# Latent attention scores as split products, with the embedded input kept in DRAM meanwhile

## The reference, cut to what matters

```python
def first_block(x, p, positions, ...):
    x = layer_norm(x, ln_emb_g, ln_emb_b)              # the "embedded input"
    z = x @ w_in[i]
    xs, gs, cq, ckv, kr, gm = jnp.split(z, IN_SPLIT_POINTS, axis=-1)
    ys = s5_branch(xs, ...) * silu(gs)
    ym = mla_branch(cq, ckv, kr, cos, sin, ...) * silu(gm)
    mix = concatenate([ys, ym]) @ w_out[i]
    u = DEEPNORM_ALPHA * x + mix                       # the embedded input again
    ple = sigmoid(u @ w_pg[i]) * (p[i] @ w_pp[i])
    return layer_norm(u + ple, ln_g[i], ln_b[i])

def mla_branch(...):                                   # 4 heads
    q = rms_norm(cq) @ w_uq                            # per head 128 plain + 64 rotary rows
    kv = rms_norm(ckv) @ w_ukv                         # per head 128 plain key rows + 128 value rows
    k_rope = rotary(kr, cos, sin)                      # 64 rows, shared by the heads
    s = einsum(q, k) * scale                           # contraction over 128 + 64 rows
    s = where(key_pos <= q_pos, s, -inf)               # causal
    return softmax(s) @ v
```

## Time and profile before

| | us |
|---|---|
| three runs | 2280.39, 2281.03, 2282.52 |
| their median | 2281.03 |
| span of the profiled execution, first to last instruction | 2278.5 |
| PE busy over the span | 2194.5 (96%) |
| DVE, ACT, POOL busy | 1154.4, 754.5, 1192.3 |

### The profile page before, as it was taken

The page is one execution under the profiler, slowest core; times in us unless marked ns, Lnnn a source line. Parts: engine busy times, 40 slices in busy tenths (PEclk is TensorE's granted clock), DMA queues, the critical chain, the costliest instruction groups (busy, mean ns, idle before and its releaser), DMA issues.

```text
span 2278.5 us, 27616 instructions
## 1 busy us (share of the span) xinstructions
PE 2194.5 (96%) x10944; PEld 1609.4 (71%) x10944; DVE 1154.4 (51%) x1473; ACT 754.5 (33%) x1161; POOL 1192.3 (52%) x809
## 2 busy tenths in 40 slices
PE   6999999999999899999999999998999999999998
PEld 2454464676886687568866788876788888888886
DVE  6950844551186611550036724775966666652434
ACT  4121042332112511650036343135555555531211
POOL 2533510204787265435656765365688888844442
PEclk8999999999999999999999999999999999999999
DMA  3336232001223422101211235233122222154111
GB/s 134 111 74 104 84 85 70 4 19 47 92 84 98 143 65 84 34 10 37 89 25 51 83 111 194 87 144 130 47 62 82 83 82 84 64 182 157 47 37 74
DMA packets 62590, 187.73 MB, mean 82 GB/s; under 512 B 14903, under 2 KB 17255, under 8 KB 62415
## 3 DMA queue, kind: packets, MB, share of 16 engines
q1 hardware_dynamic: 50688, 143.30, 19.6%
q10 hardware_dynamic: 8688, 32.26, 3.8%
q0 software_dynamic: 3088, 10.43, 2.4%
HBM read 150.15 MB, written 33.59 MB: 81 GB/s over the span
## 4 chain that ended last, share of the span: by engine, by line
PE 89%; DVE 5%; ACT 3%; issue 2%; POOL 1%; DMA 1%; ACTq 0%; DVEq 0%
PE ps L3005 21%; PE ps L2651 16%; PE ps L2616 14%; PE ps L3124 10%; PE ps L2929 4%; PE ps L3038 3%; PE ps L325 3%; PE ps L3076 2%; PE ps L493 1%; PE ps L481 1%; PE ps L348 1%; PE ps L2731 1%; PE ps L607 1%; PE ps L618 1%; PE ps L630 1%
## 5 line engine op out<-in xcount | busy, mean ns | idle before, releaser
L1390 POOL TENSOR_TENSOR w_parts<-front,sb_zero 128x1024 fp32r<-128x1024 f32 x69 | 139.0, 2014 | 300.8 <-PE ps L3124 117.7
L3124 PE MATMUL ps<-ffn_parts,w_parts 128*128 128x512 f32 x1008 | 230.3, 389 | 1.5 <-DVE front L2577 1.5
L1463 POOL TENSOR_TENSOR up_parts<-front,up_parts 128x512 fp32r<-128x512 f32 x120 | 194.5, 1629 | 69.5 <-ACT up_parts L1736 69.5
L2616 PE MATMUL ps<-front 128*128 128x512 f32 x512 | 225.5, 599 | 2.7 <-ACT front L892 2.7
L1395 POOL TENSOR_TENSOR w_parts<-front,w_parts 128x1024 fp32r<-128x1024 f32 x75 | 207.6, 2769 | 22.5 <-ACT w_parts L1891 7.5
L3124 PEld LDWEIGHTS ps<-ffn_parts,w_parts 128*128 128x128 f32 x1008 | 189.0, 188 | 41.7 <-issue 2.6
L1300 POOL TENSOR_TENSOR front<-front,sb_csilu 128x1024 f32<-128x1024 f32 x48 | 104.3, 2172 | 210.5 <-DMA front<-w_ada 210.5
L3005 PE MATMUL ps<-t_high,up_parts 128*128 128x512 f32 x640 | 204.8, 391 | 4.9 <-ACT back L1743 4.9
L2651 PE MATMUL ps<-h_high,w_parts 128*128 128x512 f32 x672 | 187.6, 394 | 0.6 <-PE ps L2929 0.6
L2616 PEld LDWEIGHTS ps<-front 128*128 128x128 f32 x512 | 96.5, 191 | 118.6 <-issue 118.1
L3005 PE MATMUL ps<-h_high,up_parts 128*128 128x512 f32 x480 | 154.5, 389 | 1.5 <-DVE back L2345 1.5
(11 more groups left out here) (399 smaller groups left out, 4510.6 us busy)
## 6 DMA issues: line engine op xcount, KB each, us to landing
front<-w_ada SPq DMA_DIRECT2D x48, 512.0 KB, 3.6
front<-w_up SPq DMA_DIRECT2D x44, 512.0 KB, 4.4
front<-w_down SPq DMA_DIRECT2D x22, 512.0 KB, 3.6
front<-w_in SPq DMA_DIRECT2D x16, 512.0 KB, 3.6
front<-w_out SPq DMA_DIRECT2D x16, 512.0 KB, 4.7
residual<-back ACTq DMA_DIRECT2D x2, 4096.0 KB, 15.6
front<-w_gates SPq DMA_DIRECT2D x16, 512.0 KB, 4.0
gates<-back SPq DMA_DIRECT2D x16, 512.0 KB, 3.2
```

The costliest lines, as they stand in the source:

```text
L1390: pool.tensor_tensor(high, raw, zero[:, 0:1].to_broadcast((P, PAGE)), ALU.add)\
L1463: pool.tensor_tensor(parts[:, BANK:], src, parts[:, 0:BANK].bitcast(F32), ALU.subtract)\
L2616: mm = pe.matmul(ps[:, bank + nt, :], ring[:, slot, at + k * step:at + k * step + P], rhs(k0 + k)[:, nt * BANK:(nt + 1) * BANK], start=sta ...
L3124: mm = pe.matmul(ps[:, 2 * m + nt, :], parts[n % 2 + w_][:, at:at + P], half_of(AR[kk % 4 + x_], nt), start=k == 0 and q == 0, stop=k == N ...
```

## The change

Scores. Each plain key and query tile now exists twice: `KNH`, `QNH` (high, copied by ACT from PSUM as `fp32r`) and `KNL`, `QNL` (low, by DVE: PSUM minus high). Each score range becomes five `fp32r` matmuls into one accumulation: QNH*KNH, QNH*KNL, QNL*KNH over 128 rows; then `QRS`*`KRH` over 128 rows, where `QRS` of a head holds the high part of its 64 rotary query rows in one half and their low part in the other, and `KRH` the high part of the rotated keys in both halves; then the high query half against `KRL`, the low part of the keys, over 64 rows. A range is at least 256 columns wide: item 0 of each head is widened from 128 to 256 columns and item 4 from 640 to 768 (the softmax still reads w columns).

Room. The low parts lie on pages 4 to 11, where `XN` is. So ACT sends `XN` to DRAM (4 MB) after the first layer norm, DVE waits for that before the first low key part, and POOL fetches it back after the last scores have been transposed (`mla_turned` 32); DVE waits for it ahead of L2219. Two pages of the later projections move (`MH[1]` from 46 to 14, `UH[2]` from 14 to 41). The zero fill of `QR` (L2172) goes.

Waits. PE reuses a bank pair in the key and query stages only when DVE's low part is made too (`k_low`, `q_low`). Several semaphores become one running count each (`ONE_COUNT`); `T(name, n)` gives the semaphore and the shifted count, and replaces `S(name), n` at each of their waits.

The diff, without the remaining lines that only put `T(...)` for `S(...)`:

```diff
@@ -55,14 +55,25 @@
 N_VEC = _at
+ONE_COUNT = {"kv_tile": ("z_tile", 16), "q_tile": ("z_tile", 28), "qr_tile": ("z_tile", 32), "glu_tile": ("z_tile", 34),
+             "pp_tile": ("z_tile", 38), "wo_tile": ("z_tile", 46), "pg_tile": ("z_tile", 54),
+             "kv_free": ("z_free", 16), "q_free": ("z_free", 28), "yg_ready": ("z_free", 32), "glu_sig": ("z_free", 36),
+             "pp_free": ("z_free", 40)}
 def program(nc, t, out):
     with ExitStack() as ctx:
         sems = {}
         def S(name):
+            name = ONE_COUNT.get(name, (name, 0))[0]
             if name not in sems:
                 sems[name] = ctx.enter_context(nc.semaphore(name))
             return sems[name]
+        def T(name, n):
+            return S(name), ONE_COUNT[name][1] + n if name in ONE_COUNT else n
...
@@ -144,9 +155,12 @@
-        QN, QR, KN = pages(28, 4), pages(32, 4), pages(36, 4)
+        QNH, QNL = rounded_pages("q_high", 28, 4), rounded_pages("q_low", 4, 4)
+        KNH, KNL = rounded_pages("k_high", 36, 4), rounded_pages("k_low", 8, 4)
+        QRS = rounded_pages("q_rot_parts", 32, 4)
+        KRH, KRL = rounded_pages("k_rot_high", 44, 1)[0], rounded_pages("k_rot_low", 46, 1)[0]
         VT = pages(40, 4).rearrange("p k (a d) -> p (k a) d", a=2)
-        KROT, CM = page(44), page(45)
+        CM = page(45)
         COS, SIN = page(48), page(49)
...
+        xn_dram = nc.dram_tensor("embedded", (P, FT, SEQ), F32, kind="Internal").ap()
...
@@ -196,9 +211,9 @@
         WR_LAST = rounded_pages("w_parts_last", 42, 2)
         WR_1 = rounded_pages("w_parts_1", 36, 4)
-        MH, ML = rounded_pages("mix_high", (15, 46, 48, 49, 42, 43, 44, 45), 8), \
+        MH, ML = rounded_pages("mix_high", (15, 14, 48, 49, 42, 43, 44, 45), 8), \
             rounded_pages("mix_low", (16, 17, 18, 19, 24, 25, 26, 27), 8)
-        UH, UL = rounded_pages("u_high", (12, 13, 14, 20, 21, 22, 23, 40), 8), \
+        UH, UL = rounded_pages("u_high", (12, 13, 41, 20, 21, 22, 23, 40), 8), \
             rounded_pages("u_low", (16, 17, 18, 19, 24, 25, 26, 27), 8)
         WR_PG = rounded_pages("w_parts_pg", (48, 49), 2)
...
@@ -436,11 +451,15 @@
                 for qb in range(8):
                     w = (qb + 1) * P
                     q = slice(qb * P, (qb + 1) * P)
-                    sc = []
-                    for c0 in range(0, w, BANK):
-                        c1 = min(w, c0 + BANK)
-                        sc.append((c0, c1, QN[:, h, q], KN[:, h, c0:c1], True, False))
-                        sc.append((c0, c1, QR[:, h, q], KROT[:, c0:c1], False, True))
+                    sc, half = [], slice(64 * (h % 2), 64 * (h % 2) + 64)
+                    wide = 256 if qb == 0 else 768 if qb == 4 else w
+                    for c0 in range(0, wide, BANK):
+                        c1 = min(wide, c0 + BANK)
+                        sc.append((c0, c1, QNH[h][:, q], KNH[h][:, c0:c1], True, False))
+                        sc.append((c0, c1, QNH[h][:, q], KNL[h][:, c0:c1], False, False))
+                        sc.append((c0, c1, QNL[h][:, q], KNH[h][:, c0:c1], False, False))
+                        sc.append((c0, c1, QRS[h][:, q], KRH[:, c0:c1], False, False))
+                        sc.append((c0, c1, QRS[h][half, q], KRL[half, c0:c1], False, True))
                     items.append((sc, CM[:, SEQ - w:SEQ], w,
                                   lambda k, h=h: VT[:, k, h * P:(h + 1) * P], P,
                                   OBUF[h % 2][:, qb, :]))
...
@@ -1354,6 +1373,8 @@
             for k in range(2):
                 pool.wait_ge(S("mla_turned"), 30 + k)
                 pool.dma_start(PT_IN[k], t["pT"][k * P:(k + 1) * P, :]).then_inc(S("p_landed"), 16)
+            pool.wait_ge(S("mla_turned"), 32)
+            pool.dma_start(XN, xn_dram).then_inc(S("xn_back"), 16)
             pool.wait_ge(S("mla_out"), 32)
             def split(b, i=0, per=0):
...
@@ -1518,6 +1539,9 @@
             norm_act(act, "ln_emb", FT, lambda k: XN[:, k, :], lambda k: XN[:, k, :],
                      lambda k: V("ln_emb_g", k), lambda k: V("ln_emb_b", k), 0, True, TEMPS_1)
+            act.wait_ge(S("norm_ready"), tiles_to("ln_emb", FT))
+            act.dma_start(xn_dram, XN).then_inc(S("xn_in_dram"), 16)
+
             def z(tile, dst, func):
                 act.wait_ge(S("z_tile"), tile + 1)
                 src = two(2 * (tile % 2))
...
@@ -1586,22 +1610,22 @@
                     latent_gain_act(act, 2)
             for m in range(4):
-                act.wait_ge(S("kv_tile"), m + 1)
-                act.activation(KN[:, m, :], two(2 * (m % 2)), ACT.Copy).then_inc(S("kv_free"), 1)
+                act.wait_ge(*T("kv_tile", m + 1))
+                act.activation(KNH[m], two(2 * (m % 2)), ACT.Copy).then_inc(S("kv_free"), 1)
             ada_read(0, 16)
             for kt in range(8):
-                act.wait_ge(S("kv_tile"), 4 + kt + 1)
+                act.wait_ge(*T("kv_tile", 4 + kt + 1))
                 act.activation(VT[:, kt, :], ps[:, kt % 4, :], ACT.Copy).then_inc(S("kv_free"), 1)
             act.wait_ge(S("y_in_dram"), 16 * STEP)
...
             for m in range(4):
-                act.wait_ge(S("q_tile"), m + 1)
-                act.activation(QN[:, m, :], two(2 * (m % 2)), ACT.Copy).then_inc(S("q_free"), 1)
+                act.wait_ge(*T("q_tile", m + 1))
+                act.activation(QNH[m], two(2 * (m % 2)), ACT.Copy).then_inc(S("q_free"), 1)
...
@@ -2169,27 +2193,37 @@
             link(dve.memset(CM, 0.0))
             dve.sem_inc(S("dve_step"), 1)
-            link(dve.memset(QR, 0.0))
+
+            dve.wait_ge(S("xn_in_dram"), 16)
+            dve.wait_ge(S("z_tile"), 16)
+            for m in range(4):
+                dve.wait_ge(*T("kv_free", m + 1))
+                dve.tensor_tensor(KNL[m], two(2 * (m % 2)), KNH[m].bitcast(F32), ALU.subtract).then_inc(S("k_low"), 1)
             dve.wait_ge(S("kr_landed"), 64)
             dve.wait_ge(S("ssm_ps"), 32)
-            tt(KROT, page(46), COS, ALU.mult)
-            tt(page(46), page(47), SIN, ALU.mult)
-            tt(KROT, KROT, page(46), ALU.add)
+            tt(page(46), page(46), COS, ALU.mult)
+            tt(page(47), page(47), SIN, ALU.mult)
+            tt(page(46), page(46), page(47), ALU.add)
+            link(dve.tensor_copy(KRH, page(46)))
+            tt(KRL, page(46), KRH.bitcast(F32), ALU.subtract)
+            for m in range(4):
+                dve.wait_ge(*T("q_free", m + 1))
+                dve.tensor_tensor(QNL[m], two(2 * (m % 2)), QNH[m].bitcast(F32), ALU.subtract).then_inc(S("q_low"), 1)
             for m in range(2):
-                dve.wait_ge(S("qr_tile"), m + 1)
+                dve.wait_ge(*T("qr_tile", m + 1))
+                tt(page(47), two(4 * m), COS, ALU.mult)
+                tt(page(22), two(4 * m + 2), SIN, ALU.mult)
+                dve.sem_inc(S("qr_free"), 1)
+                tt(page(47), page(47), page(22), ALU.add)
                 for i in range(2):
-                    h = slice(64 * i, 64 * i + 64)
-                    tt(QR[h, 2 * m + i, :], two(4 * m)[h, :], COS[h, :], ALU.mult)
-                tt(page(46), two(4 * m + 2), SIN, ALU.mult)
-                dve.sem_inc(S("qr_free"), 1)
-                for i in range(2):
-                    h = slice(64 * i, 64 * i + 64)
-                    tt(QR[h, 2 * m + i, :], QR[h, 2 * m + i, :], page(46)[h, :], ALU.add)
+                    own, other = slice(64 * i, 64 * i + 64), slice(64 - 64 * i, 128 - 64 * i)
+                    link(dve.tensor_copy(QRS[2 * m + i][own, :], page(47)[own, :]))
+                    tt(QRS[2 * m + i][other, :], page(47)[own, :], QRS[2 * m + i][own, :].bitcast(F32), ALU.subtract)
             dve.sem_inc(S("dve_step"), 1)
             def gated(m):
-                dve.wait_ge(S("glu_sig"), m + 1)
+                dve.wait_ge(*T("glu_sig", m + 1))
                 tt(page(20 + m % 2), page(20 + m % 2), YF[:, m, :], ALU.mult)
             def gated_state(m):
...
@@ -2214,8 +2248,9 @@
             for k in range(4):
                 dve.wait_ge(S("gm_high"), k + 1)
                 dve.tensor_tensor(ML[4 + k], GM[:, k, :], MH[4 + k].bitcast(F32), ALU.subtract).then_inc(S("gm_split"), 1)
+            dve.wait_ge(S("xn_back"), 16)
             for m in range(8):
-                dve.wait_ge(S("wo_tile"), m + 1)
+                dve.wait_ge(*T("wo_tile", m + 1))
                 dve.scalar_tensor_tensor(XN[:, m, :], XN[:, m, :], ALPHA, two(2 * (m % 2)),
                                          ALU.mult, ALU.add).then_inc(S("u_ready"), 1)
             for k in range(8):
...
@@ -2745,32 +2780,36 @@
             block_landed(B_UKV)
             for m in range(4):
                 if m >= 2:
-                    pe.wait_ge(S("kv_free"), m - 1)
+                    pe.wait_ge(*T("kv_free", m - 1))
+                    pe.wait_ge(S("k_low"), m - 1)
                 tile(2 * (m % 2), b % RING, lambda k: CKV, kts=1, at=m * P).then_inc(S("kv_tile"), 1)
```

(52 more changed lines are left out.)

## The result

The changed kernel takes 2284.76 us (median of 15 runs, 2282.82 to 2286.11), the kernel before on the same chip 2280.75 us (15 runs, 2278.19 to 2282.52). The ratio is 1.0018 [1.0010, 1.0026]: 4.0 us slower by the medians. By the ratio's interval that is slower by 0.1 to 0.3%. The profiled executions are 2281.2 and 2278.5 us long, 2.7 us apart. The profiled execution of the changed kernel took 2283.47 us and is one of the six shorter ones of its fifteen (2282.82 to 2284.18 us, mean granted clock 0.988 or 0.989); the other nine took 2284.54 to 2286.11 us at 0.985 or 0.986.

The account below looks back on a forecast made before the run. PE was taken to bound the kernel (89% of the chain of waits). Attention -0.9, key stage +2.3 and query stage +1.3 sum to +2.7 us: span 2281.2, plus 2.5 from span to median, 2283.7 us; range 2272 to 2294.

Parts of the forecast that it names:

- Matmul prices: Attention scores: fp32r matmuls cost 0.229 us at 512 columns, 0.175 at 384, 0.120 at 256; 17.9 us back.
- The switch: Scores' fifth matmul, 64 rows between 128: 0.39 us per range for changing row count, 48 ranges, 18.7 us.
- Attention: Scores +0.8 us in sum, less 1.7 us hidden in PE's idle time at head changes: -0.9 us.
- Item 0's rise: First score item of a head grows from 0.43 to 0.99 us, hidden in idle time at three head changes: -1.7.
- Key stage: PE waits for DVE's subtraction before reusing bank pairs; the values start at 333.1 instead of 330.8: +2.3 us.
- Query wait: After the fourth query tile PE waits for DVE's subtraction (1.22 + 0.1 us) beyond ACT's copy: +1.3 us.
- The embedded input: Transfer to DRAM until 60 us, back near 527 us, both hidden with 6 and 30 us of cover: nothing.
- DVE's longer way: DVE's rotary writes grow some 3 us a pair, ending near 380; attention needs them at 400: hidden.
- a free switch: Rival, scores: row-count changes cost nothing for fp32r, giving 18.7 us, 2265.0 us; chance 0.10.
- dear narrow matmuls: Rival, scores: fp32r matmuls under 512 columns are no cheaper than 512, 10.9 us more, 2294.6 us; chance 0.13.
- a late transfer: Rival, embedded input: late weight block near 60 us or late return adds up to 10 us; chance 0.03.
- The half price: Rival, scores: only the drain shows at a row-count change, load hidden, 9.4 us less, 2274.3 us; chance 0.12.

Follow-up runs that it names:

- the round trip alone: The kernel before with only the embedded input's way out to DRAM and back added: 2280.75 us, ratio 1.0001 to the kernel before.
- values early: The changed kernel with the first two value tiles waiting only for the third low key part, the third for the fourth: 2280.93 us.
- rotary tile early: The changed kernel with the first rotary tile waiting only for the third low query part, its second half for the fourth: 2282.30 us.
- the last experiment: The changed kernel with 128-row fifth matmul, early rotary tile, three bank pairs, and state-space output regrouped by row count: 2257.81 us, 0.9910 to the kernel before.

## Why the prediction was right

The forecast was 2283.7 us and the same within 0.2%; 2284.8 came out, and the profiled span on the forecast's 2281.2. That the span agrees to 0.1 us is luck: errors of 1.6 and 1.7 us cancelled, and two small differences outside the forecast (-0.66 ahead, +0.6 behind) did too. The 2.5 us that the forecast added to the span was the median less the span of one execution. In the runs on record each time is 2.0 to 2.2 us above its own span for the kernel before, and 2.2 to 2.3 for the changed one. Point by point:

- Matmul prices: right. 0.23 at 512 columns, 0.175 to 0.177 at 384, 0.118 at 256, as assumed from the earlier trace rows. From their first start to the transposes items 4 to 7 take 2.51, 2.51, 2.78 and 3.09 us; 2.53, 2.53, 2.80 and 3.07 follow from the forecast's prices. They agree so well because the first record of an item takes 0.08 more than its price and the switches less than theirs: without switches the same items take 1.84, 1.84, 2.12 and 2.40 (the kernel with 128 rows throughout).
- The switch: right in kind, too dear by 1.6 us. Between two ranges it is 0.10 before the fifth record and 0.30 spread over the next two starts, 0.39 to 0.40, as the earlier trace rows said; 512 and 256 columns hardly differ. At an item's end, where transposes follow, it is 0.34. So 16 x 0.39 + 32 x 0.34 = 17.1 us and not 18.7.
- Attention: -2.5 us, -0.9 forecast. The line above gives the 1.6 us between them by count; smaller terms that cancel aren't separated, such as the first three items, which take 0.4 us longer up to DVE's gating (7.79 for 7.39) and hide the first head's switches. Item 0's rise went into the idle time at the change of head, as forecast: 0.22 us by the record is left of 0.70.
- Key stage: right, +2.33 for +2.3, with the waits where they were put. Query wait: right, +1.26 for +1.3.
- Value tiles: missed. "The values ... start at 333.1: +2.3 us" left out that the clock falls behind that wait: +1.67 us, shown by starting them early. The forecast attended to what the idle time was, not to what it does to the work after it. This is why the rotary tiles start 4.6 us later and not 3.6.
- The embedded input: right, nothing. DVE's longer way: right, hidden; its last rotary write ends at 381.2 and attention needs it at 401.
- The rivals: a free switch is excluded by the starts above, dear narrow matmuls by the run without widening, a late transfer by the round trip alone. The half price asked for the load to stay hidden, but a pair costs 0.39, and the weight loads below show that the load is held. The other estimate of the forecast, 0.053 us a switch, is a third of the price or less.

Of what the prediction said would show it, the gaps at the switches, the values' start (2.33 us later, counted from the key stage's start), attention's end (518.57 for 518.5) and the return before 530 stood in the trace. Rotary tiles came 4.6 us later and not 3.6, and attention started at 401.26 and not 400.3: both are the 1.67 of the clock less the 0.66 at the start. The transposes after a change of head still had 0.22 us of idle time.

## What to carry to other kernels

Count the places where TensorE goes from one row count to another, and price each pair at 0.34 to 0.39 us from such a row of the kernel's own trace; if a matmul's rows can be filled up with harmless or wanted data, or the short ones put side by side, the price goes (14 us by filling up; 6 to 8 us by putting side by side, in each of two places). Leaving half of the rows out of the fifth matmul saved nothing. Where an edit makes PE wait in a row of short tiles, look at the granted clock of the next microseconds too: the wait of 2.46 us brought 1.67 us with it, and three bank pairs for two removed both.

## What the runs showed of the hardware

- A switch between 128 and 64 rows costs the same for fp32r and plain 32-bit data, with 128, 256 or 512 columns: 0.20 on the way in or out, 0.39 to 0.40 the pair. It shows as a later start of the switched record (0.09 to 0.10) and of the one after it (0.10). The weight loads (PEld) show that the load doesn't run ahead across a switch. Between 128-row matmuls a load starts 0.23 us ahead of its own matmul, beside the one before it. On the way in and on the way out it starts with its own matmul's record, after idle time (the changed kernel, where the fifth and the sixth record start at 451.38 and 451.80):

```profile
451.38 0.18 PEld L340 LDWEIGHTS ps<-k_rot_low,q_rot_parts 64*128 64x128 f32 x1 [0.37 <-issue]
...
451.80 0.19 PEld L340 LDWEIGHTS ps<-k_high,q_high 128*128 128x128 f32 x1 [0.24 <-issue]
```

  In the kernel with 128 rows throughout, the same load stands 0.23 ahead of its matmul, which starts at 444.10. How the 0.20 us divide between the held load and the rest, no run measured.

```profile
443.87 0.19 PEld L340 LDWEIGHTS ps<-k_rot_low,q_rot_parts 128*128 128x128 f32 x1
```

- fp32r matmuls go in proportion to their columns from 512 down to 256 (0.229 to 0.118), and at 128 stay at 0.109 to 0.115, which is also the pace of transposes and outputs.
- The clock fell behind like waits in one trace and not in another. At attention's start all kernels wait for DVE. The granted clock falls to about 0.6 there in three of the traces: values early (401 to 405 us, 0.62), rotary tile early (408 to 412, 0.58) and the last experiment (389 to 393, 0.60). In the other eight it stays at 1.00. With the values early nothing is lost by it: attention ends 3.7 us earlier, all that had been gained before it. With the rotary tile early attention takes 118.82 us for 117.31.
